# Grouped heads' input products as three passes of split operands, split during the latent products; output matrix loaded later

## What is computed

```python
h = _layernorm(jnp.concatenate([meta, x], axis=1), ln_emb_g, ln_emb_b)      # 528 x 1024
z = jnp.einsum('bld,dc->blc', h, w_in)                                      # 528 x 1472
q_a, kv_a, k_pe, q_g, k_g, v_g = jnp.split(z, IN_OFFSETS, axis=-1)          # 256 128 64 | 512 256 256
qg = axial(_rmsnorm(q_g.reshape(B, L, GQA_HEADS, GQA_DIM), g_q_gqa))        # 4 heads of 128
kg = axial(_rmsnorm(k_g.reshape(B, L, GQA_KV_HEADS, GQA_DIM), g_k_gqa))     # 2 heads
vg = v_g.reshape(B, L, GQA_KV_HEADS, GQA_DIM)
```

## Time and profile before

| | before |
|---|---|
| median of 3 runs | 2297.98 us (2297.66 to 2299.71) |
| profiled execution, its own time | 2298.23 us |
| its span | 2296.4 us |
| busy share of the span | PE 97%, PEld 79%, DVE 72%, ACT 53%, POOL 20% |
| mean granted clock of TensorE | 0.991 |
| input products (first block to the first latent product behind them) | 15.9 to 113.3 us |
| attention of the first block begins | 139.3 us |

### The profile page before, as it was taken

The page is one execution under the profiler, slowest core; times in us unless marked ns, Lnnn a source line. Parts: engine busy times, 40 slices in busy tenths (PEclk is TensorE's granted clock), DMA queues, the critical chain, the costliest instruction groups (busy, mean ns, idle before and its releaser), DMA issues.

```text
span 2296.4 us, 29195 instructions
## 1 busy us (share of the span) xinstructions
PE 2238.6 (97%) x10544; PEld 1825.0 (79%) x10544; DVE 1661.1 (72%) x1592; ACT 1222.6 (53%) x1240; POOL 465.7 (20%) x362
## 2 busy tenths in 40 slices
PE   8999999999999999999999999889999999999998
PEld 4668877888888888888888888778877778888886
DVE  2647689988999999999999999782557546433434
ACT  2135347676777767768677677643344532422320
POOL 4042139962111112211111112110220010000000
PEclk9999989999999999999999999999999999999999
DMA  7030169999999999999999999962221232223220
GB/s 277 3 104 1 58 231 364 399 379 382 370 394 380 374 399 375 387 384 377 395 376 382 389 378 377 322 217 99 62 87 37 110 129 92 95 89 110 82 102 37
DMA packets 141390, 551.58 MB, mean 240 GB/s; under 512 B 11536, under 2 KB 12688, under 8 KB 124224
## 3 DMA queue, kind: packets, MB, share of 16 engines
q1 hardware_dynamic: 128240, 507.29, 57.5%
q0 software_dynamic: 10592, 38.41, 6.5%
q10 hardware_dynamic: 2480, 4.80, 0.6%
HBM read 522.66 MB, written 25.69 MB: 239 GB/s over the span
## 4 chain that ended last, share of the span: by engine, by line
PE 88%; DVE 6%; POOL 2%; issue 1%; ACT 1%; DMA 1%; DVEq 0%; SPq 0%; ACTq 0%; POOLq 0%
PE PS L395 84%; PE PS L733 1%; PE PS L682 1%; DVE low L2115 1%; ACT act L1813 1%; POOL act L2780 1%; DVE ring_parts L2383 1%; DVE st L1903 1%; PE PS L566 1%; DVE small L2470 1%; DVE act L1930 0%; DMA acc_d<-act,to_c 0%; POOL xs L2764 0%; PE PS L1035 0%; POOL act L2782 0%
## 5 line engine op out<-in xcount | busy, mean ns | idle before, releaser
L395 PE MATMUL PS<-act_parts 128*128 128x512 f32 x3388 | 1068.5, 394 | 9.0 <-issue 7.5
L2115 DVE TENSOR_TENSOR low<-ring,act_parts 128x2048 fp32r<-128x2048 f32 x380 | 856.9, 2308 | 33.0 <-ACT act_parts L1547 33.0
L395 PEld LDWEIGHTS PS<-act_parts 128*128 128x128 f32 x3388 | 635.9, 189 | 141.1 <-issue 9.0
L1547 ACT ACTIVATE act_parts<-ring 128x2048 fp32r<-128x2048 f32 x384 | 707.6, 1912 | 16.9 <-PE PS L395 9.3
L395 PE MATMUL PS<-low,act_parts 128*128 128x512 f32 x1584 | 618.3, 390 | 0.0
L395 PE MATMUL PS<-act_parts,ring_parts 128*128 128x512 f32 (+1 forms) x1344 | 397.3, 383 | 0.0
L395 PEld LDWEIGHTS PS<-low,act_parts 128*128 128x128 f32 x1584 | 298.2, 188 | 60.3
L395 PEld LDWEIGHTS PS<-act_parts,ring_parts 128*128 128x128 f32 x1344 | 248.1, 188 | 58.7 <-issue 10.7
L395 PE MATMUL PS<-ring_parts,act_parts 128*128 128x512 f32 x1088 | 262.1, 393 | 3.2 <-DVE act_parts L2547 2.1
L395 PE MATMUL PS<-ring_parts 128*128 128x512 f32 (+1 forms) x672 | 255.5, 380 | 0.0
L395 PEld LDWEIGHTS PS<-ring_parts,act_parts 128*128 128x128 f32 x1088 | 205.1, 189 | 49.2 <-issue 3.5
(11 more groups left out here) (279 smaller groups left out, 1854.1 us busy)
## 6 DMA issues: line engine op xcount, KB each, us to landing
ring<-w_gate_up SPq DMA_DIRECT2D x264, 1024.0 KB, 8.8
ring<-w_down SPq DMA_DIRECT2D x132, 1024.0 KB, 8.1
ring<-w_ff SPq DMA_DIRECT2D x16, 2048.0 KB, 7.7
ring<-w_in SPq DMA_DIRECT2D x12, 2048.0 KB, 8.1
ring<-w_o SPq DMA_DIRECT2D x1, 4096.0 KB, 24.0
ring<-w_out SPq DMA_DIRECT2D x2, 2048.0 KB, 8.5
acc_d<-ring POOLq DMA_DIRECT2D x5, 512.0 KB, 6.7
act<-x SPq DMA_DIRECT2D x4, 512.0 KB, 5.2
```

What stands on the lines that cost most here:

```text
L395: return eng.matmul(o, lhsT, rhs, start=first, stop=last, **kw)
L1547: A_(W1hi[c % CS], W1[c], ACT.Copy).then_inc(sem["high"], 1)
L2115: tt(W1lo[c], W1[c], W1hi[c % CS].bitcast(F32), ALU.subtract).then_inc(sem["low"], 1)
```

## The change

The products of the grouped heads (blocks 6 to 13 and the five value blocks) become three passes of split operands: HThi with the high part of the weights, HThi with the low part, HTlo with the high part. ACT makes the high parts: eight copies of HT (128 x 528) behind raw(0), and eight of the weights (w_high, 128 x 1024 each), four of them between the copies of the latent blocks, two behind raw(7), two behind job 2. DVE makes the low parts, in place of the float32 values: w_low(0) to (3) behind square(1), then the eight of HT once block 5 is done, w_low(4) and (5) ahead of scale(0), and w_low(6) and (7) in job 4. TensorE does the two high passes of blocks 6 and 7 first and the low passes of both behind them; the sum of job 0 comes after block 7, as before. HThi and the high weights stand where w_o was loaded; so w_o's load moves behind the last value block and the partner copies, ahead of the expert pieces. The signal order of two semaphores is extended. Nothing else changes.

```diff
--- before.py
+++ after.py
@@ -91,11 +91,11 @@
     "turned_gains": [("oT_out", 8), ("o2T_lo", 8)],
     "residual_dve": [("mix", 16), ("y_lo", 2), ("summed", 8), ("mix2", 8), ("ff_out", 16)],
     "routing_dve": [("lam_dot", 2), ("tile_routed", 3 * 4), ("based", 8)],
-    "lists_dve": [("first_hot", 8), ("list_hot", 8), ("bias_lo", 2), ("gated", 1), ("tokens_listed", 1), ("places_listed", 1),
+    "lists_dve": [("wq_lo", 4), ("hT_lo", 8), ("wkv_lo", 4), ("first_hot", 8), ("list_hot", 8), ("bias_lo", 2), ("gated", 1), ("tokens_listed", 1), ("places_listed", 1),
                   ("gates_listed", 1), ("over_named", 3), ("over_added", 4), ("over_listed", 3)],
     "routing_pool": [("sel_made", 1), ("bias_one", 1), ("bias_padded", 1), ("extras", 1),
                      ("gates_split", 1), ("bd_low", 1), ("extra_of", 1), ("over_made", 4)],
-    "lists_act": [("token_hot", 4), ("bias_hi", 2), ("bd_high", 1), ("gates_high", 2)],
+    "lists_act": [("hT_hi", 8), ("wq_hi", 4), ("wkv_hi", 4), ("token_hot", 4), ("bias_hi", 2), ("bd_high", 1), ("gates_high", 2)],
     "biased_dve": [("sa_biased", 16), ("sb_masked", 16)],
     "added": [("pos_in", 16)],
     "places_dve": [("placed", 4)],
@@ -206,6 +206,13 @@
         qg_partner = partner_rows[:, 0:HG * S].rearrange("p (h s) -> p h s", h=HG)
         kg_partner = partner_rows[:, HG * S:].rearrange("p (h s) -> p h s", h=HKV)
         w_in_s = ring[:, 0:KD * ZCOLS].rearrange("p (k c) -> p k c", k=KD)
+        w_in_lo = ring_parts[:, 0:KD * ZCOLS].rearrange("p (k c) -> p k c", k=KD)
+        HThi = [ring_parts[:, at:at + L] for at in [16384 + k * L for k in range(KD - 1)] + [23040]]
+        HTlo = nc.alloc_sbuf_tensor_at("HTlo", [P, KD * L], F32R, offset=act_at + 4 * 5120)[:, :].rearrange(
+            "p (k c) -> p k c", k=KD)
+        wz_hi = [ring_parts[:, 12288 + u * 1024:12288 + (u + 1) * 1024].rearrange("p (k c) -> p k c", k=KD)
+                 for u in range(HG)]
+        wv_hi = ring_parts[:, 14336:16384].rearrange("p (k c) -> p k c", k=KD)
         oThi = ring_parts[:, 8192:8192 + KD * S].rearrange("p (k s) -> p k s", k=KD)
         oTlo = [part(9216, 4, S), part(22528, 4, S)]
         wqb = ring[:, 20480:22016].rearrange("p (k c) -> p k c", k=2)
@@ -446,6 +453,26 @@
                     ins = mm(PS[0:w, b, 0:b_ - a], w_in_s[:, k, c:c + w], HT[:, k, a:b_], k == 0, k == KD - 1)
                 ins.then_inc(put("z_psum", b), 1)
 
+            def split_block(n, high_x):
+                c, w, a, b_ = zb[n]
+                hi, last = wz_hi[(n - 6) if n < 10 else (n - 10) // 2], n < 10
+                if high_x:
+                    b = next_bank()
+                    eng.wait_ge(*free[b])
+                    free[b] = past("z_raw", n + 1)
+                    eng.wait_ge(*past("hT_hi", KD))
+                    eng.wait_ge(*(past("wq_lo", n - 5) if n < 10 else past("wkv_lo", (n - 10) // 2 + 1)))
+                    for k in range(KD):
+                        mm(PS[:, b, 0:b_ - a], hi[:, k, :], HThi[k][:, a:b_], k == 0, False)
+                        mm(PS[:, b, 0:b_ - a], w_in_lo[:, k, c:c + w], HThi[k][:, a:b_], False, False)
+                    put("z_psum", b)
+                else:
+                    b = where["z_psum", n + 1]
+                    for k in range(KD):
+                        eng.wait_ge(*past("hT_lo", k + 1))
+                        ins = mm(PS[:, b, 0:b_ - a], hi[:, k, :], HTlo[:, k, a:b_], False, k == KD - 1)
+                    ins.then_inc(sem["product_psum"], 1)
+
             def sum_squares(j):
 
                 eng.wait_ge(*past("squared", j + 1))
@@ -469,16 +496,22 @@
                 free[b] = past("rope_sin", n + 1)
                 mm(PS[0:m.shape[0], b, 0:w], m, src).then_inc(put("rope_psum", b), 1)
 
-            for n in range(7):
+            for n in range(6):
                 z_block(n)
                 if n == 0:
                     turn_meta()
                 if n == 1:
                     eng.wait_ge(*past("hT_dve", 5))
             eng.wait_ge(*past("mats_in", 16))
-            for j in range(7):
-                z_block(7 + j)
+            for high_x in (True, False):
+                split_block(6, high_x)
+                split_block(7, high_x)
+            sum_squares(0)
+            for j in range(1, 7):
+                for high_x in (True, False):
+                    split_block(7 + j, high_x)
                 sum_squares(j)
+            eng.wait_ge(*past("wkv_lo", 4))
             eng.wait_ge(*past("zero_rows", 4))
             for n in range(2):
                 partner(n)
@@ -487,9 +520,11 @@
                 b = next_bank()
                 eng.wait_ge(*free[b])
                 free[b] = past("vg_raw", t + 1)
+                rows = slice(t * P, t * P + n)
                 for k in range(KD):
-                    ins = mm(PS[0:n, b, 0:HKV * VDIM], HT[:, k, t * P:t * P + n], w_in_s[:, k, ZVG:ZCOLS],
-                             k == 0, k == KD - 1)
+                    mm(PS[0:n, b, 0:HKV * VDIM], HThi[k][:, rows], wv_hi[:, k, :], k == 0, False)
+                    mm(PS[0:n, b, 0:HKV * VDIM], HThi[k][:, rows], w_in_lo[:, k, ZVG:ZCOLS], False, False)
+                    ins = mm(PS[0:n, b, 0:HKV * VDIM], HTlo[:, k, rows], wv_hi[:, k, :], False, k == KD - 1)
                 ins.then_inc(put("vg_psum", b), 1)
                 if t < 4:
                     sum_squares(7 + t)
@@ -1258,14 +1293,13 @@
             eng.dma_start(wkvb, A["w_kv_b"][0]).then_inc(signal("wq_in", 16), 16)
             eng.dma_start(v(22752, 2, L, parts=ROPE), A["c_rope_m"]).then_inc(signal("rope_in", 16), 16)
             eng.dma_start(v(23808, 2, L), A["c_rope_g"]).then_inc(signal("rope_in", 16), 16)
-            eng.dma_start(w_o_s, A["w_o"][0].rearrange("(k p) c -> p k c", p=P)).then_inc(signal("wo_in", 16), 16)
-
             eng.wait_ge(*past("z_psum", 14))
             eng.wait_ge(*past("vg_psum", 5))
             eng.wait_ge(*past("normed", 11))
             for at in range(0, P, 32):
                 eng.dma_start(partner_rows[at:at + 32, :], gqa_rows[at ^ 32:(at ^ 32) + 32, :]).then_inc(
                     signal("partners_in", 16), 16)
+            eng.dma_start(w_o_s, A["w_o"][0].rearrange("(k p) c -> p k c", p=P)).then_inc(signal("wo_in", 16), 16)
             for c in range(3):
                 eng.dma_start(chunk_place(c), chunk_src(0, c)).then_inc(sem[f"expert_in{c}"], 16)
 
@@ -1444,12 +1478,44 @@
                     eng.wait_ge(*past("normed", j - 1))
                 A_(rb[:, j % 2, 0:w], b[:, 0:w], ACT.Sqrt, scale=1.0 / dim, bias=EPS_1).then_inc(signal("rms_std"), 1)
 
+            def w_high(u):
+                if u < HG:
+                    eng.wait_ge(*past("w_in1", 16))
+                    A_(wz_hi[u], w_in_s[:, :, ZQG + u * P:ZQG + (u + 1) * P], ACT.Copy).then_inc(signal("wq_hi"), 1)
+                elif u < HG + HKV:
+                    eng.wait_ge(*past("w_in2", 16))
+                    eng.wait_ge(*past("z_psum", u + 3))
+                    eng.wait_ge(*past("wq_lo", u - 3))
+                    A_(wz_hi[u - HG], w_in_s[:, :, ZKG + (u - HG) * P:ZKG + (u - HG + 1) * P], ACT.Copy).then_inc(
+                        signal("wkv_hi"), 1)
+                else:
+                    ks = slice(4 * (u - 6), 4 * (u - 5))
+                    eng.wait_ge(*past("z_psum", 10))
+                    eng.wait_ge(*past("wq_lo", 4))
+                    A_(wv_hi[:, ks, :], w_in_s[:, ks, ZVG:ZCOLS], ACT.Copy).then_inc(signal("wkv_hi"), 1)
+
             eng.wait_ge(*past("zero_rows", 4))
-            for n in range(7):
+            raw(0)
+            eng.wait_ge(*past("hT_dve", 5))
+            for k in range(KD):
+                if k % 2 == 0:
+                    eng.wait_ge(*past("hT_act", k // 2 + 1))
+                A_(HThi[k], HT[:, k, :], ACT.Copy).then_inc(signal("hT_hi"), 1)
+            raw(1)
+            for n in range(2, 6):
+                w_high(n - 2)
                 raw(n)
-            for j in range(7):
+            raw(6)
+            raw(7)
+            w_high(4)
+            w_high(5)
+            rms_std(0)
+            for j in range(1, 7):
                 raw(7 + j)
                 rms_std(j)
+                if j == 2:
+                    w_high(6)
+                    w_high(7)
             for t in range(5):
                 n = P if t < NT else META
                 eng.wait_ge(*past("vg_psum", t + 1))
@@ -2026,10 +2092,39 @@
                     eng.wait_ge(*past("rope_done", n - 1))
                 tt(o, x, s_, ALU.mult).then_inc(signal("rope_sin"), 1)
 
+            def w_low(u):
+                if u < HG:
+                    eng.wait_ge(*past("wq_hi", u + 1))
+                    c = slice(ZQG + u * P, ZQG + (u + 1) * P)
+                    tt(w_in_lo[:, :, c], w_in_s[:, :, c], wz_hi[u].bitcast(F32), ALU.subtract).then_inc(
+                        signal("wq_lo"), 1)
+                    return
+                eng.wait_ge(*past("wkv_hi", u - 3))
```

(21 more changed lines are left out.)

## The result

The changed kernel takes 2302.05 us (median of 20 runs, 2300.07 to 2304.75) against 2299.11 (20 runs, 2296.93 to 2301.13) for the one before: a ratio of 1.0014, 95% interval 1.0008 to 1.0020. That is a loss of some 3 us, less than the 0.2% taken as the bound for no change. The forecast was no change at 2300.3 us, in a range of 2291.5 to 2305.

What follows compares the result with a forecast made beforehand. The prediction took PE (97% busy) to bound the kernel in the touched stage. A base of +0.7 and a clock loss of 1.4 made +2.1 us on 2298.23, about 2300.3 us, range 2291.5 to 2305.

Steps and rivals of the forecast that it cites:

- The saving of PE: Grouped and value blocks: three split passes replace full-precision products, saving 5.7 + 2.4 + 2.9 = 11.0 us if PE never waits.
- The turns: Before block 7's end: DVE and POOL two-operand operations alternate, last hT_lo ready at 61.9, block 7 ending 63.9 against 58.8.
- DVE keeps its turn: Rival: queued DVE operations pass without POOL turns between, latent products start at 106.1, -7.2 us, 2291.0 us; chance 0.13.
- Block 7 and the clock: Block 7 ends at 63.9; PE's waits lower its clock until about 65, costing 1.4 us more.
- the 3 and the 16 us of the earlier trace: Two earlier places where the granted clock stood at 0.50: some 3 us of dense work, and 16 us from 298 to 314.
- The slower rival: PE's clock stays low until 70 or longer; low until 72 costs 5.7 us, about 2304; chance 0.19.
- DVE's chain: From rms_std(0) to job 8: first reciprocal at 68.1 (+6.6), later ones +2.2 and +1.6, squares of job 8 ending at 103.8.
- The sum: Whole kernel: 0.7 + 1.4 = +2.1 us on 2298.23, so about 2300.3.
- The base: Input stage without the clock's loss: first latent query product at 114.05 instead of 113.32, +0.7 us.
- the late output matrix: Its load goes out at some 119 us, lands by 143 to 150, first read at 201.51: costs nothing.
- passes might be no cheaper: Rival: grouped products keep 0.86 us a group, +6.4 us, with the clock +7.8, 2306; chance 0.04.
- the signs named: Trace marks for right or wrong, among them DVE without idle time of more than 2.5 us from 68 to 104.

Runs made afterwards that it cites:

- experiment 9: The changed kernel with POOL's residual operations paced by DVE's reciprocals and w_low(6), (7) moved from DVE to POOL: 2291.62 us, ratio 0.9967 to the kernel before.
- experiment 1: The changed kernel without POOL's eight residual operations, signals kept, so the result is wrong: ratio 1.012 to the kernel before, stage 90.46 us.
- experiment 2: The changed kernel with POOL's eight residual operations released one by one as DVE begins a reciprocal: 2293.37 us, ratio 0.9974 to the kernel before.
- experiment 8: The changed kernel with each POOL residual operation of 1024 elements split into two of 512: 2298.01 us, ratio 0.9996 to the kernel before.
- experiment 6: The changed kernel with 11, 11 and 6 idle PE products ahead of the waits for hT_lo(1), (2) and (3): 2299.71 us, ratio 1.0001 to the kernel before.
- experiment 4: The kernel before with only the output matrix's load moved behind the partner copies: 2299.53 us, ratio 1.0001 to the kernel before.
- experiment 3: The kernel before, float32 products kept, with POOL's eight residual operations paced by DVE's squares: 2299.50 us, ratio 0.9999 to the kernel before.
- experiment 7: The changed kernel with the high passes of blocks 6 to 9 ahead of the low passes of 6 and 7: 2297.63 us, ratio 0.9993 to the kernel before.
- experiment 5: The changed kernel with nine idle PE products ahead of each wait for the second and third hT_lo: 2300.47 us, ratio 1.0005 to the kernel before.

## Why the prediction was right

**The saving of PE (11.0 us if it never waits): right.** A sum and a block of 512 go from 72.73 to 78.74 in the changed kernel, 6.01 us against 5.89 in the prediction; a sum and a value block from 105.61 to 108.99, 3.38 against 3.33. In experiment 9, where PE waits only once behind the first low pass (0.98 us at 94.42), 9.7 us of it arrive.

**The turns: right in kind, and so close partly by luck.** w_low(3) was to end at 49.8, and the first hT_lo begins at 49.95; hT_lo(2) at 58.5, and PE is released by it at 58.45; the last at 61.9, and it ends at 62.05. Three small errors largely cancel in this. POOL's first residual operation began 0.43 us later than in the kernel before (34.14 against 33.71); each pair of turns was shorter than worked out (3.33 with a w_low and 2.77 with an hT_lo against 3.4 and 2.9); and the last step was added up wrong, since 59.2 and five hT_lo of 0.6 are 62.2 and not 61.9. This step rested on a single pair of rows, and experiments 1, 2 and 8 bear it out: take POOL's operations away, move them or halve them, and the wait goes, goes or is halved. Experiment 8 rules out a share in proportion to data. The Trainium skill (SBUF — State Buffer, Who interferes with whom) tells of one engine that holds the pair while the other waits; this agrees with every row of these turns, all between operations with two tensor operands; the last section shows an operation of POOL for which it doesn't hold. The rival put beside it (DVE keeps its turn) fell: its stage of some 90.2 us came out only where POOL's operations were gone or moved (90.46 and 90.49).

**Block 7 and the clock: right in kind, with two errors that cancel.** 63.9 and 1.4 for the clock make 65.3, measured 65.45. At full clock block 7 would have ended at 62.05 + 2.25 = 64.3 by experiment 6, 0.4 later than the 63.9. The clock was at 0.50 from 58 to 64 and back at full speed after 66, near the 65 of the prediction. That 65 was a choice between the 3 and the 16 us of the earlier trace rows, not worked out, so that it hit is luck. The clock's price was 1.15 us by experiment 6, not 1.4. The slower rival, a clock low until 70, did not come.

**DVE's chain: right, a little late at each step.** First reciprocal 69.50 (68.1 and 1.4), then 80.01 (78.2 and 1.4), 83.95 (82.2 and 1.4), the squares of job 8 at 105.55 (103.8 and 1.4). The last three are some 0.35 late: a sum with a block of 512 is 0.12 dearer than worked out, and PE does two of them ahead of the reciprocal at 80.01. The idle times took back most of the first delay, as said, and w_low(6), (7) were not given back.

**The sum: +2.1 predicted, +2.45 in the stage.** The base was +0.7 and is 1.3, mostly by the lateness of DVE's chain, the clock was 1.4 and is 1.15. The total is 2302.05 against 2300.3: of the 1.75 us that are missing, 0.9 are the kernel before itself, whose median in the larger number of runs is 2299.11 and not the 2298.23 on which the sum stood, 0.35 are the stage, and the 0.5 left are within the scatter of the expert loop. That the late output matrix costs nothing was right (experiment 4), and that passes might be no cheaper was not so. Of the signs named, one was missed by a hair: DVE idled 2.53 us ahead of the reciprocal at 80.01, where at most 2.5 was said.

**What the prediction didn't ask.** It took POOL's order as given. POOL's residual operations have no reader in this stage, and starting them later turns the loss of 3 us into a gain of 6 (experiment 2). Behind "By itself it would fit in the 25 us that DVE idles" the prediction asked what else lies there, and found POOL; it didn't ask whether that work must lie there.

## What to carry to other kernels

An idle stretch of DVE is free for work with two SBUF operands only if POOL has no such work there. Walk both engines by turns, one operation each, each turn as long as the other's operation. Long POOL operations that nobody waits for belong beside DVE's reciprocals or behind the stage. Where they can't move, halving them shortens each wait (from 2.27 to 1.20 us here) and gave 3.7 us of the stage back. Changing PE's order gave 4.4 us back, but starting the chain on time gave 9.4, and some 12 with two operations taken off the chain.

## What the runs showed of the hardware beyond that

POOL's operation with one tensor operand and a scalar held DVE only at its start. Two of them ran one behind the other in every kernel, some 2.8 us each where nothing held them, just when DVE was due to square the first two copied blocks. In the changed kernel the first square began together with POOL's second operation, at 31.20; in experiment 3 the squares began 0.94 us behind it. DVE in the changed kernel, then POOL and DVE in experiment 3:

```profile
31.21 2.18 DVE L2060 TENSOR_TENSOR act<-act 128x512 f32<-128x512 f32 x2 [7.08 <-ACT act L1462]
...
31.35 2.79 POOL L2608 TENSOR_SCALAR act<-act 128x1024 f32<-128x1024 f32 x1
...
32.29 1.29 DVE L1994 TENSOR_TENSOR act<-act 128x512 f32<-128x512 f32 x2 [7.08 <-ACT act L1428]
```

Two squares took 2.18 us in the one and 1.29 in the other, though POOL's operation ran on over both. The whole delay is in the first square: in the changed kernel it took 1.58 us, against 0.68 for one without POOL (82.25), and ended at 32.79, which is 1.59 behind the start of POOL's operation. In the kernel before, where POOL's second operation began at 30.77 and the square at 31.35, it ended at 32.37, 1.60 behind that start; in experiments 1, 7 and 8 it was 1.59 each time. Where DVE's square began first (experiments 5 and 6, by 0.07 and 0.03 us), POOL's operation was the one that stood: it took 3.25 and 3.30 us. So these rows fit a DVE that is stopped for the first 0.9 us of POOL's 2.79 and free from then on. Why, no run shows.

The reciprocals weren't slowed at all beside POOL's operations with two tensor operands: 3.34 us at 80.18 in experiment 9, where POOL's w_low ran from 80.34 to 82.73, as in the rows of DVE alone. So pacing is free beside a reciprocal of 512 columns, which is longer than POOL's 2.35. Beside one of 264 (1.80) it isn't: in experiment 2 the scale behind the one at 67.14 took 1.02 instead of 0.49, as expected there.
